# Branch products: where the convolution's high and low parts are made

## The reference

```python
y_a = short_conv_mixer(c_b, c_c, c_x, conv_w[layer]) @ w_branch_a[layer]
attn = dsa_attention(q..., k, v, iq..., ik, iw, rel_bias)
y_b = attn @ w_branch_b[layer]
gates = jax.nn.sigmoid(jnp.concatenate([g_a, g_b], axis=-1) + b_gate[layer])
merged = gates[..., :D_MODEL] * y_a + gates[..., D_MODEL:] * y_b
x = x + merged @ w_out[layer]
```

## Time and profile before

| what | value |
|---|---|
| median of 3 runs | 2690.65 us (2688.7 to 2692.6) |
| the profiled execution's own time | 2683.23 us |
| its span, first to last instruction | 2681.4 us |
| TensorE busy | 2521.8 us, 94% of the span |
| VectorE busy | 1708.9 us, 64% |
| ScalarE busy | 970.5 us, 36% |
| GpSimd busy | 633.3 us, 24% |
| mean granted TensorE clock | 0.976 |

### The profile page before, as it was taken

The page is one execution under the profiler, slowest core; times in us unless marked ns, Lnnn a source line. Parts: engine busy times, 40 slices in busy tenths (PEclk is TensorE's granted clock), DMA queues, the critical chain, the costliest instruction groups (busy, mean ns, idle before and its releaser), DMA issues.

```text
span 2681.4 us, 31860 instructions
## 1 busy us (share of the span) xinstructions
PE 2521.8 (94%) x12136; PEld 2079.0 (78%) x12136; DVE 1708.9 (64%) x2896; ACT 970.5 (36%) x1749; POOL 633.3 (24%) x473
## 2 busy tenths in 40 slices
PE   5999999888999899999999989999999988999888
PEld 3778888677787688888888867888778767778877
DVE  5499999477424887886644378558676564009933
ACT  4431222477223332222411243333242254228732
POOL 2147522476543000000000220000000144324433
PEclk7999999999999999999999999999999989999999
DMA  4112233100455266564623222332364115232143
GB/s 166 44 37 67 79 94 98 48 1 17 162 172 146 87 189 194 174 187 135 228 79 110 67 91 87 105 100 79 102 259 149 52 51 173 79 103 71 44 146 102
DMA packets 260706, 293.17 MB, mean 109 GB/s; under 512 B 10856, under 2 KB 216140, under 8 KB 260556
## 3 DMA queue, kind: packets, MB, share of 16 engines
q1 hardware_dynamic: 260556, 291.14, 33.6%
HBM read 223.95 MB, written 66.10 MB: 108 GB/s over the span
## 4 chain that ended last, share of the span: by engine, by line
PE 64%; DVE 27%; ACT 5%; DMA 2%; issue 1%; POOL 1%; SPq 0%; DVEq 0%; ACTq 0%; POOLq 0%
PE ps L67 63%; DVE sm L100 6%; DVE m L97 6%; ACT tmp L73 2%; DVE tmp L103 2%; DVE tmp L79 2%; DVE sm L79 2%; PE ps L70 1%; DVE tmp L76 1%; DVE p2l L76 1%; ACT pth L73 1%; DVE wl L76 1%; DVE pwa L76 1%; DVE B2l L76 1%; DVE X L79 0%
## 5 line engine op out<-in xcount | busy, mean ns | idle before, releaser
L76 POOL TENSOR_TENSOR wl<-raw,wh 128x512 fp32r<-128x512 f32 (+1 forms) x224 | 292.9, 1329 | 1623.0 <-ACT wh L73 1622.9
L73 ACT ACTIVATE wh<-raw 128x512 fp32r<-128x512 f32 (+1 forms) x388 | 226.5, 621 | 256.5 <-PE ps L67 179.9
L73 ACT ACTIVATE tmp<-ps 128x512 f32<-128x512 f32 (+5 forms) x172 | 127.4, 751 | 391.3 <-PE ps L67 376.5
L67 PE MATMUL ps<-B2h,wh 128*128 128x512 f32 x616 | 244.0, 396 | 13.0 <-DVE B2l L76 6.7
L67 PE MATMUL ps<-B2h,wl 128*128 128x512 f32 x616 | 241.5, 392 | 0.0
L67 PE MATMUL ps<-B2l,wh 128*128 128x512 f32 x616 | 241.2, 392 | 0.0
L76 DVE TENSOR_TENSOR tmp<-tmp,ps 128x512 f32<-128x512 f32 x204 | 138.5, 685 | 107.5 <-PE ps L67 91.4
L67 PE MATMUL ps<-ah,wh 128*128 128x512 f32 (+1 forms) x608 | 191.9, 392 | 14.0 <-DVE xt L85 9.9
L73 ACT ACTIVATE wh<-ws 128x512 fp32r<-128x512 f32 x152 | 94.4, 626 | 290.8 <-DVE ws L76 263.6
L67 PE MATMUL ps<-B3h,wh 128*128 128x512 f32 x448 | 178.4, 398 | 16.6 <-DVE B3l L76 7.5
L67 PE MATMUL ps<-al,wh 128*128 128x512 f32 (+1 forms) x608 | 190.6, 390 | 0.0
(11 more groups left out here) (282 smaller groups left out, 5850.7 us busy)
## 6 DMA issues: line engine op xcount, KB each, us to landing
ada<-in_ada_w SPq DMA_DIRECT2D x48, 512.0 KB, 3.7
raw<-in_w_in SPq DMA_DIRECT2D x37, 512.0 KB, 4.5
raw<-in_a_w_in SPq DMA_DIRECT2D x33, 512.0 KB, 4.5
gates<-tmp SPq DMA_DIRECT2D x32, 512.0 KB, 3.0
raw<-in_w_ffn_gate SPq DMA_DIRECT2D x24, 512.0 KB, 6.0
hd<-tmp SPq DMA_DIRECT2D x22, 512.0 KB, 4.5
gf<-hd SPq DMA_DIRECT2D x22, 512.0 KB, 6.8
raw<-in_a_w_out SPq DMA_DIRECT2D x20, 512.0 KB, 3.5
```

What stands on the lines that cost most here:

```text
L67: return self.e.matmul(*a, **k) if self.e else Ins()
L73: return self.e.activation(*a, **k) if self.e else Ins()
L76: return self.e.tensor_tensor(*a, **k) if self.e else Ins()
```

## The change

ScalarE makes `ch0` to `ch3` inside the attention's pipeline, at the step of `turned(63)` and behind it, so ahead of `stored(63)`. They wait for `("top", 63)` (the last reads of the mask and the table) and each for its load `("chl", j)`, and no longer for `ATTENDED`. A helper `conv_lo` makes a low part on the engine it is given: VectorE makes `cl0` and `cl1` as soon as `("pv", 31)` is there, ahead of `ol0` to `ol3`; GpSimd, which still waits for `ATTENDED`, makes `cl2` and `cl3`. The events are the same, those of `cl0` and `cl1` now on VectorE's semaphore.

```diff
@@ act_attend
-        pipeline(64, [(4, turned), (2, norm), (7, stored), (0, exps)])
+        def conv(n):
+
+            if n < 63:
+                return
+            e.wait_ge(*self.at("top", 63))
+            for j in range(4):
+                e.wait_ge(*self.at("chl", j))
+                e.activation(self.ch[j][:, :], self.tmp[(self.CH + j) % 5][:, :], ACT.Copy).then_inc(
+                    self.sig["ahi"].up(("chi", j)), 1)
+
+        pipeline(64, [(4, turned), (2, norm), (7, stored), (0, exps), (4, conv)])
@@ act_branch
         for j in range(4):
-            e.wait_ge(*self.at("chl", j))
-            e.activation(self.ch[j][:, :], self.tmp[(self.CH + j) % 5][:, :], ACT.Copy).then_inc(
-                self.sig["ahi"].up(("chi", j)), 1)
-        for j in range(4):
             e.activation(self.oh[j][:, :], self.OT[:, j * S:j * S + S], ACT.Copy).then_inc(
@@
+    def conv_lo(self, e, j, signal):
+
+        e.wait_ge(*self.at("chi", j))
+        e.tensor_tensor(self.cl[j][:, :], self.tmp[(self.CH + j) % 5][:, :], self.ch[j][:, :].bitcast(F32),
+                        ALU.subtract).then_inc(signal.up(("clo", j), ("tfree", self.CH + j)), 1)
+
     def dve_branch(self, e):
         vec = self.sig["vec"]
+        e.wait_ge(*self.at("pv", 31))
+        for j in range(2):
+            self.conv_lo(e, j, self.sig["vlo"])
         for j in range(4):
             e.wait_ge(*self.at("ohi", j))
@@ pool_branch
-        for j in range(4):
-            e.wait_ge(*self.at("chi", j))
-            e.tensor_tensor(self.cl[j][:, :], self.tmp[(self.CH + j) % 5][:, :], self.ch[j][:, :].bitcast(F32),
-                            ALU.subtract).then_inc(self.sig["plo"].up(("clo", j), ("tfree", self.CH + j)), 1)
+        for j in range(2, 4):
+            self.conv_lo(e, j, self.sig["plo"])
```

## The result

The changed kernel takes 2682.3 us (median of 10 runs, 2677.97 to 2685.08), the kernel before 2689.09 us (median of 10, 2686.7 to 2692.6): ratio 0.9976, 95% interval [0.9967, 0.9985], so 4.0 to 8.9 us faster. The forecast was 2686.5, in 2684.0 to 2690.7, with 0.22 on faster by over 0.2%. The measured time lies under the range. The gain forecast, 4.1 us, lies at the lower end of the interval.

What follows compares the result with a forecast made beforehand. Four GpSimd subtractions in a row were taken to bound the first branch product's start. Its fourth step would move from 686.48 to 682.35, 4.1 us off: 2690.65 - 4.1 = 2686.5 us, range 2684.0 to 2690.7.

Steps and rivals of the forecast that it cites:

- step 4: Start of the first branch product's fourth step on TensorE, counted from the last value product's end; forecast 4.1 us earlier.
- the sentence on the port: VectorE and GpSimd: the exclusion rule leaves the sum the same here and is worth more in "the second rival".
- the turns: VectorE and GpSimd subtractions alternate by whole instructions; a `cl` takes 2.35 us alone, 3.34 beside `ol`.
- rival 1: Convolution loads land sooner, so `ot` is not held up: gain 5.5 us, 2685.2 us; chance 0.14.
- Rival 2: TensorE's clock falls late, at the first branch product's fourth step: gain only 0.5 us, 2690.1 us; chance 0.14.
- Rival 3: On ScalarE, copies waiting for a late last load hold up `ot`: 1.5 us slower, 2692.2 us; chance 0.05.
- Rival 4: Something behind the branch's start takes the gain back, such as VectorE's order at gated products: 2690.6 us; chance 0.08.

Runs made afterwards that it cites:

- the two repeats: The changed kernel, unchanged, measured a second and a third time beside the kernel before: ratios 0.9977 and 0.9982.
- loads_reordered: The changed kernel with the convolution's four loads and high-part copies in the order 0, 2, 3, 1: ratio 0.9986 to the kernel before.
- lows_only: The changed kernel with the high parts left behind `ot`, low parts still two on VectorE and two on GpSimd: ratio 0.9968 to the kernel before.
- four_lows_only: The kernel before with all four low parts made on VectorE, the high parts staying behind `ot`: ratio 0.9976 to the kernel before.
- before_busy: The kernel before with 16 extra products on TensorE between the last value product and the first branch product: ratio 1.0000 to the kernel before.
- highs_only: The changed kernel with all four low parts back on GpSimd, so only the high parts moved: ratio 1.0000 to the kernel before.
- four_on_vector: The changed kernel with all four low parts on VectorE and none on GpSimd: ratio 0.9969 to the kernel before.

## Why the prediction missed, point by point

**The chain and its sum: right.** Four traces of the changed kernel's order have step 4 at 8.8, 9.2, 9.0 and 9.1 us, 3.9 to 4.3 us earlier than before, where 4.1 was forecast. Term by term in the trace after, with its 0.5 us offset taken off: GpSimd starts at 676.3 (forecast 676.5), its pair takes 5.69 (2.36 + 3.35 = 5.71), VectorE's two 2.36 (2.44), TensorE starts after 1.41 (1.4), the last load lands in 6.6 (6.7). The four traces also bear out that step 4 hangs on that load: it lands 6.6, 6.8, 6.9 and 7.0 us after its issue, and step 4 follows at 8.8, 9.0, 9.1 and 9.2. One slip: the sentence on the port points to the second rival, but it is the first that uses the turns.

**What was missed: the level of before, and the room for scatter.** The step that failed is "so I take the difference over: 2690.65 - 4.1 = 2686.5". The 2690.65 is the median of three runs. Ten runs gave 2689.09 and 98 gave a mean of 2687.7, so that base was 1.6 to 3 us high, and single runs of before reach from 2682.65 to 2693.08. On the base measured beside it, the same sum gives 2689.1 - 4.1 = 2685.0; the measured 2682.3 is 2.7 under that. So the base alone doesn't account for the miss: the whole range moved down by 1.6 would begin at 2682.4. Its lower end left 1.2 us under rival 1's 2685.2 and should have allowed for two medians of a kernel whose runs have a standard deviation of 2.3 us.

**How much is left to explain.** The changed kernel itself has 27 runs now, mean 2682.4, against 98 of before, mean 2687.7: 5.3 us, give or take 1.1. But the level of before differs from one comparison to the next (means of 2686.5 to 2689.2), and the changed kernel was not timed beside the lowest. With each comparison taken against its own runs of before, the 27 give 5.8 us, give or take 1.2, and the 17 runs of the two repeats alone 5.2, give or take 1.4. So of the 2.7 us some 1 to 1.6 was scatter of the first comparison, and 1.1 to 1.7 more than the trace shows remains.

It is not in this kernel alone. Of the nine kernels with an earlier step 4, eight gained more than step 4 shows, by 0.6 to 5.2 us from the table's ratios, and loads_reordered 1.7 less. A fit over all thirteen comparisons, each with its own level of before and with step 4's change counted in full, puts 1.2 us on top for these nine, give or take 0.8. It doesn't go with the fall of the clock in the long wait (lows_only and four_lows_only have both the fall and the excess, before_busy has neither the fall nor a gain), and no run tells what it goes with: whether it is a small real saving, and where, stays open. The traces can't find it: from step 4 to the end of the span they take 1991.3 to 1999.3 us with the same instructions, in the mean 1996.5 in the five whose step 4 is at 13.1 us or later and 1996.1 in the nine others.

**Rival 1, the loads land sooner.** It didn't happen by itself. loads_reordered made it happen, and its 7.6 us (forecast for the rival: 681.0 - 673.36 = 7.6) show that the turns between the engines were worked out rightly. Here the Trainium skill ("SBUF — State Buffer", Who interferes with whom) agrees: a VectorE instruction with two SBUF inputs and a GpSimd one that reads SBUF exclude each other for the whole instruction, as they did here (3.42 us on VectorE against 1.23 alone). Splitting work between these two engines buys little: all four on VectorE beat two and two by 3.2 to 3.6 us at step 4, and by 2.0 where both have the reordered loads (5.6 against 7.6).

**Rival 2, the clock.** No trace of the changed kernel shows a fall between 660 and 700, in spite of three waits of 1.41, 1.10 and 1.68 us. The swing that the Trainium skill describes ("TensorE: Matmul & The Clock Gate", A second HAM failure mode) was not seen there. But the clock elsewhere is what made the range too narrow: I looked for it only where the change is.

**Rival 3, the hold-up of `ot`.** The mechanism is real: highs_only has only that part and is 1.8 us later at step 4. That is less than the 2.6 expected, mostly because the last load landed 1.0 us after the last value product there and not 1.6. **Rival 4** is out: for the 366 products from step 4 on TensorE has no new wait.

**The version to keep** is four_on_vector, alone or with the reordered loads (0.9969 and 0.9965): TensorE waits for nothing after its first step. There the moved high parts pay as well, 3.2 us at step 4 (5.6 against 8.8 in four_lows_only, of which 1.6 is the low clock in that trace, by the 7.2 expected at full clock), while beside two low parts on GpSimd they gave 0.5 to 0.9 (8.8 to 9.2 against 9.7).

## What to carry to other kernels

Work on the start of the one instruction that the chain hangs on, and measure it from the last event that the change doesn't touch: that number repeated to 0.4 us where whole executions scattered by 10. When four short operations feed a chain, give them to the engine that does each faster than the consumer uses it up (here a new one starts every 1.14 us in four_on_vector, against steps of 1.36), and don't share them with an engine that locks it out. Before an operation is moved into an idle stretch, check when its input lands, and what stands behind it in the queue. And before a range is written, ask how far two medians of the same kernel lie apart.

## What the runs showed of the hardware

The granted clock of TensorE fell at different places from one execution to the next, with the same instructions: 0.75 and 0.59 over 520 to 545, and 0.971 to 0.978 over whole spans of the kernel before. On a kernel in which TensorE is busy 94% of the time this moved the end of identical code at 673 us by up to 7.8 us, while the stretches without a low clock repeated to 0.9 us in sum. VectorE and GpSimd held each other off in whole instructions whichever came first: 1.23 and 2.36 us alone, 3.42 and 3.35 in turn. Three loads of 512 KB issued 0.4 to 0.5 us apart, with two more right behind, took 5.0, 5.8 and 6.6 us to land in the trace after and 5.1, 5.9 and 6.7 in that of before; over the twelve traces with this order the last one took 5.9 to 7.2.
